# The experts' stage of a transformer kernel on one core: 40 loaded expert units in slot order against 32 units, of which eight serve two token slots

## The reference, cut to what matters

```python
g_sel = argmax(softmax(t @ w_rg + b_rg))           # one of 4 groups per token
e_prob = softmax((t @ w_re + b_re)[g_sel])         # 8 experts in the group
top_p, top_i = top_k(e_prob, 2)
combine = g_p * top_p / sum(top_p)                 # per token, over 32 experts
for e in range(32):                                # expert width 256
    hid = silu(t @ w_gate[e]) * (t @ w_up[e])
    out += combine[:, e] * (hid @ w_down[e])
```

## Time and profile before

| | |
|---|---|
| median of 3 runs (lowest to highest) | 2045.34 us (2042.76 to 2045.85) |
| the profiled execution | 2042.77 us, its span 2041.0 us |
| mean granted clock of PE in it | 0.989 of full |
| PE / POOL busy over the span | 96% / 65% |
| DMA over the span | 473.92 MB, mean 232 GB/s |
| from the first gather to the last unit's silu | 246.1 to 680.9 us |

### The profile page before, as it was taken

How to read it: one execution, slowest core, us unless ns; L and a number is a source line. 1 busy time by engine, 2 the same in 40 slices (tenths; PEclk the granted TensorE clock), 3 DMA queues, 4 the chain that set the end, 5 groups by cost and what they waited for, 6 DMA issues and landing times.

```text
span 2041.0 us, 34520 instructions
## 1 busy us (share of the span) xinstructions
PE 1968.1 (96%) x13902; PEld 1768.6 (87%) x13902; DVE 1020.0 (50%) x2154; ACT 824.4 (40%) x874; POOL 1329.9 (65%) x310
## 2 busy tenths in 40 slices
PE   6999889999999999999999999899999999999998
PEld 4879767667676799999999769799999999999998
DVE  6767474558565465455336334453335334654212
ACT  4343354444444553334434332443344333434332
POOL 5727157776768668777775412377777777777884
PEclk8999899999999999999999999999999999999999
DMA  8537198989898655666665402156665666655552
GB/s 354 214 124 289 67 374 349 376 345 368 355 375 336 230 224 210 244 239 225 241 241 205 153 33 104 60 215 242 247 239 204 233 233 244 229 221 192 185 185 83
DMA packets 67414, 473.92 MB, mean 232 GB/s; under 512 B 8064, under 2 KB 9184, under 8 KB 10208
## 3 DMA queue, kind: packets, MB, share of 16 engines
q1 hardware_dynamic: 65344, 466.82, 60.2%
q10 hardware_dynamic: 1952, 5.44, 0.7%
HBM read 471.18 MB, written 1.05 MB: 231 GB/s over the span
## 4 chain that ended last, share of the span: by engine, by line
PE 48%; issue 23%; POOL 19%; DMA 6%; DVE 1%; ACT 1%; SPq 0%; POOLq 0%; ACTq 0%; DVEq 0%
POOL W L632 15%; PE bank L703 11%; PE bank L705 11%; PE bank L704 11%; DMA raw<-in_pages 6%; PE bank L1197 4%; POOL YC L685 2%; PE bank L709 2%; PE bank L711 2%; PE bank L710 2%; PE bank L737 1%; ACT W L1616 1%; PE bank L728 1%; PE bank L748 1%; POOL W L685 1%
## 5 line engine op out<-in xcount | busy, mean ns | idle before, releaser
L632 POOL TENSOR_TENSOR W<-raw,W 128x2048 fp32r<-128x2048 f32 x220 | 1014.0, 4614 | 518.9 <-ACT W L1494 518.8
L703 PE MATMUL bank<-YH,W 128*128 128x256 f32 x1936 | 551.2, 285 | 1.1 <-POOL W L632 0.8
L705 PE MATMUL bank<-YH,W 128*128 128x256 f32 x1936 | 547.7, 283 | 0.0
L704 PE MATMUL bank<-YL,W 128*128 128x256 f32 x1936 | 547.6, 283 | 0.0
L1494 ACT ACTIVATE W<-raw 128x2048 fp32r<-128x2048 f32 x220 | 420.1, 1909 | 302.0 <-PE bank L705 275.6
L703 PEld LDWEIGHTS bank<-YH,W 128*128 128x128 f32 x1936 | 371.0, 192 | 3.9 <-POOL W L632 1.2
L704 PEld LDWEIGHTS bank<-YL,W 128*128 128x128 f32 x1936 | 371.3, 192 | 0.4 <-issue 0.2
L705 PEld LDWEIGHTS bank<-YH,W 128*128 128x128 f32 x1936 | 371.2, 192 | 0.0
L1828 DVE SCALAR_TENSOR_TENSOR bank<-mraw,CA,bank 128x256 f32<-128x256 f32 x696 | 329.1, 489 | 20.3
L1925 DVE TENSOR_TENSOR bank<-bank,SIL 128x256 f32<-128x256 f32 x110 | 47.6, 433 | 540.9 <-ACT SIL L1513 540.9
L703 PE MATMUL bank<-HH,W 128*128 128x256 f32 x880 | 249.7, 284 | 0.5 <-DVE HL L1927 0.4
(11 more groups left out here) (353 smaller groups left out, 3159.5 us busy)
## 6 DMA issues: line engine op xcount, KB each, us to landing
raw<-in_pages SPq DMA_DIRECT2D x299, 1024.0 KB, 4.9
mraw<-in_mpages SPq DMA_DIRECT2D x98, 1024.0 KB, 6.9
R<-in_pages SPq DMA_DIRECT2D x24, 1024.0 KB, 5.8
XR<-in_pages SPq DMA_DIRECT2D x17, 1024.0 KB, 5.5
R<-in_mpages SPq DMA_DIRECT2D x4, 1024.0 KB, 16.3
HT<-in_acts ACTq DMA_DIRECT2D x1, 1024.0 KB, 14.1
CT<-in_mpages SPq DMA_DIRECT2D x1, 1024.0 KB, 19.4
raw<-in_mpages SPq DMA_DIRECT2D x1, 1024.0 KB, 25.1
```

The source lines that it names most:

```text
L632: nc.gpsimd.tensor_tensor(WL[:, p % SLOTS, :], raw[:, p % SLOTS, :], WH[:, p % SLOTS, :].bitcast(f32), ALU.subtract).then_inc(s_lo, 1)
L703: mm(out, w[0], x[0], start=start, stop=False, skip_group_check=True)
L704: mm(out, w[0], x[1], start=False, stop=False, skip_group_check=True)
L705: return mm(out, w[1], x[0], start=False, stop=stop, skip_group_check=True)
```

## The change

The slots are numbered anew. The group with the most tokens always has slots 0 and 1; the other three groups have slots 2, 3 and 4. There are 32 units, and `JOBS` lists 40 pairs of unit and slot: units 0 to 7 run for slot 0 and then slot 1 (jobs 0 to 15), units 8 to 31 for one slot each (jobs 16 to 39). The tokens of slots 0, 1 and 2 are gathered in the start, so three gathered slots are held. Slot 1 sums its output in banks 5 and 6. The modulation pages move: one in each job from 1 to 15, then one in every second job from 17 to 35. For the first 15 their product is put in bank `TURN`, and `turn_hid` of jobs 1 to 15 waits until `mod_take` has read it. Slots 0 and 1 are scattered together, with eight matmuls in place of four. The core of the diff:

```diff
-NUNIT = GSLOTS * NE8
-MOD_UNITS = [_u for _u in range(36) if _u % 10 not in (0, 4, 7)]
+NUNIT = NEXP
+JOBS = [(_u, _j) for _u in range(NE8) for _j in range(2)] + [(_u, 1 + _u // NE8) for _u in range(NE8, NUNIT)]
+NJOB = len(JOBS)
+DONE_AT = {_u: _t for _t, (_u, _j) in enumerate(JOBS)}
+MOD_JOBS = list(range(1, 16)) + list(range(17, 37, 2))
...
-        EARLY = [(u, part) for u in range(2) for part in range(2)]
+        EARLY = [(0, 0), (0, 1)]
...
-        BY_VECTOR = [(2, 1)] + [(u, 1) for u in range(3, 36) if u not in MOD_UNITS]
-        BY_POOL = [(u, part) for u in range(2, NUNIT) for part in range(2) if (u, part) not in BY_VECTOR]
+        BY_VECTOR = [(u, 1) for u in range(NE8 + 2, NUNIT - 2, 2)]
+        BY_POOL = [(u, part) for u in range(1, NUNIT) for part in range(2) if (u, part) not in BY_VECTOR]
...
+        def mod_bank(m, i=0):
+            return PS[TURN if isinstance(i, int) and 0 <= m + 1 - MOD_AT["moe"] < 15 else MODB]
...  (SP)
-                    if u > 2:
-                        sp.wait_ge(s_gdown, u - 2)
+                    if u > 2:
+                        sp.wait_ge(s_gdown, DONE_AT[u - 3] + 1)
...
+                if u > 1:
+                    for t in range(NJOB):
+                        if JOBS[t][0] == u - 1 and t in MOD_JOBS:
+                            mod_page(MOD_AT["moe"] + MOD_JOBS.index(t))
...  (PE)
+            def turn_hid(t):
+                pe.wait_ge(s_ghid, t + 1)
+                pe.wait_ge(s_ght, t)
+                if t == 0:
+                    pe.wait_ge(s_auxd, 6)
+                if t in MOD_JOBS and t <= 15:
+                    pe.wait_ge(s_modev, MOD_AT["moe"] + MOD_JOBS.index(t))
                 for j in range(2):
                     last = nc.tensor.transpose(PS[TURN][:, j * P:(j + 1) * P], HID[:, j, :], IDENT[:])
                 last.then_inc(s_gturn, 1)
...
-            gather(0, 0)
-            gather(0, 1)
+            for j in range(2):
+                gather(j, 0)
+                gather(j, 1)
             aux(0)
+            aux(1)
+            for t in range(NJOB):
+                u, j = JOBS[t]
+                e = u % NE8
+                if t == 0:
+                    early_gate_up(0)
+                    early_gate_up(1)
+                    gather(2, 0)
+                    gather(2, 1)
+                    aux(2)
                 else:
+                    gate_up(t, range(0, KD // 2))
+                    turn_hid(t - 1)
+                    gate_up(t, range(KD // 2, KD))
+                    down(t - 1)
+                if j > 1 and 1 <= e <= 4:
+                    scatter(j - 2, e - 1)
+                if t in MOD_JOBS:
+                    k = MOD_JOBS.index(t)
                     mod_product(MOD_AT["moe"] + k - 1, 0, 1 if k < MOE_ADA else 2)
...  (ACT)
                 if u > 1:
-                    act.wait_ge(s_gu, u - 1)
+                    act.wait_ge(s_gu, DONE_AT[u - 2] + 1)
...
+                if t == 0:
+                    gathered_hi(2, 0)
+                    gathered_hi(2, 1)
+                    expert_split(1, 0)
+                    expert_split(1, 1)
+                if DONE_AT[u] == t and u + 2 < NUNIT:
                     expert_split(u + 2, 0)
                     expert_split(u + 2, 1)
...  (DVE)
+            aux_copy(1)
+            onehot(2)
+                if t in MOD_JOBS:
+                    k = MOD_JOBS.index(t)
                     vectors = (0,) if k < MOE_ADA else (1, 2)
                     mod_sum(MOD_AT["moe"] + k, vectors)
                     mod_take(MOD_AT["moe"] + k - 1, 0, len(vectors))
```

More of the change, by code:

```diff
@@ L125, in build @@
         HT = sb("HT", [P, KD, S])
+        with nc.sbuf_tensor("CTR", [P, KD * S], f32r) as CTR:
+            pass
         CT = sb("CT", [P, KD, S])
@@ L678, in _ @@
                 .then_inc(sem("iota"), 1)
-            for u in range(2, NUNIT):
+            for u in range(1, NUNIT):
                 for part in range(2):
@@ L1107, in aux, with to_tokens @@
                 for t in range(TB):
-                    last = mm(ps[:, S:S + NE8], EM[:, t, :], CW8[:, t, :], start=(t == 0), stop=(t == TB - 1),
+                    last = mm(ps[:, S:S + NE8], EM[j % 2][:, t, :], CW8[:, t, :], start=(t == 0), stop=(t == TB - 1),
                               skip_group_check=True)
                 last.then_inc(s_aux, 1)
-            def to_tokens(ps, j, r):
+            def to_tokens(ps, slots, r):
                 for b in range(2):
                     k = 2 * r + b
[L1115 to L1118, removed]
-                return last
@@ L1121, in scatter @@
-            def scatter(j, r):
+                    for j in slots:
+                        for part in OS[j]:
+                            last = mm(ps[:, b * S:(b + 1) * S], part[:, k * P:(k + 1) * P], ET[:, j % 3, :],
+                                      start=(j == slots[0] and part is OS[j][0]), stop=(j == slots[-1] and part is OS[j][1]),
+                                      skip_group_check=True)
+                return last
+            def scatter(g, r):
+                slots = (0, 1) if g == 0 else (g + 1,)
@@ L1187, in turn_hid, with down @@
                 last.then_inc(s_gturn, 1)
-            def down(u):
-                pe.wait_ge(s_ght, u + 1)
+            def down(t):
+                u, slot_j = JOBS[t]
+                pe.wait_ge(s_ght, t + 1)
                 pe.wait_ge(sem(f"expert_down_in_{u % 2}"), 16 * (u // 2 + 1))
-                if u % NE8 == 0 and u:
-                    pe.wait_ge(s_osl, 2 * (u // NE8))
+                if u % NE8 == 0:
+                    if slot_j == 1:
+                        pe.wait_ge(s_xl, 6)
+                    if slot_j > 1:
+                        pe.wait_ge(s_osl, 2 if slot_j == 2 else 2 * slot_j)
                 w = down_page(u)
@@ L1208, in _ @@
             pe.wait_ge(sem("tokens_copied"), 4)
-            gather(0, 0)
-            gather(0, 1)
+            for j in range(2):
+                gather(j, 0)
+                gather(j, 1)
             aux(0)
-            for u in range(NUNIT):
-                if u > 1:
-                    gate_up(u, range(0, KD // 2))
-                    turn_hid(u - 1)
-                    gate_up(u, range(KD // 2, KD))
-                    down(u - 1)
-                else:
-                    early_gate_up(u, 0)
-                    if u:
-                        turn_hid(u - 1)
-                    early_gate_up(u, 1)
-                    if u:
-                        down(u - 1)
-                if u in MOD_UNITS:
-                    k = MOD_UNITS.index(u)
+            aux(1)
+            for t in range(NJOB):
+                u, j = JOBS[t]
+                e = u % NE8
[5 more added lines that the diff above has]
+                    aux(2)
+                else:
+                    gate_up(t, range(0, KD // 2))
[6 more added lines that the diff above has]
+                    k = MOD_JOBS.index(t)
                     mod_product(MOD_AT["moe"] + k - 1, 0, 1 if k < MOE_ADA else 2)
-                j, e = u // NE8, u % NE8
-                if j and 1 <= e <= 4:
-                    scatter(j - 1, e - 1)
-                if j + 1 < GSLOTS:
+                if 1 < j < GSLOTS - 1:
                     if e in (5, 6):
@@ L1235, in _ @@
                         aux(j + 1)
-                if u == NUNIT - 3:
-                    pe.wait_ge(s_scd, 4 * (GSLOTS - 1))
+                if t == NJOB - 3:
+                    pe.wait_ge(s_scd, 4 * (GSLOTS - 2))
                     norm(2)
-            turn_hid(NUNIT - 1)
-            down(NUNIT - 1)
+            turn_hid(NJOB - 1)
+            down(NJOB - 1)
             def mid_norm(name, u, n):
@@ L1684, in _ @@
             after(PA["ctx_ff"] - SLOTS)
-            hid_copy(NUNIT - 1)
+            hid_copy(NJOB - 1)
             after(PA["ctx_ff"] - 1)
```

291 lines of the change are left out of this document (148 added, 143 removed).

## The result

The changed kernel took 2031.18 us in the median of 8 runs (2029.74 to 2036.25), the kernel before 2042.53 in 8 runs beside it (2038.91 to 2046.38): a ratio of **0.9948, 95% interval 0.9935 to 0.9961**, 11.4 us faster. Two more sets gave 0.9955 [0.9938, 0.9973] and 0.9948 [0.9930, 0.9966], that is 7.8 and 11.2 us. One run of the kernel before, in the set of part 4, took 3893 us and is left out of every figure.

A forecast was written before the change was run, and what follows sets the result against it. PE was taken as the bound. Start +5.8, work -7.0 and waits 12.3 in place of 16.3 (-4.0) gave -5.2 us: from the median 2045.3 to 2040.1 us, range 2033 to 2049.

The forecast's parts named there:

- What bounds, and what a gain can be: Experts' loop: PE is the bound; nothing done to the loads can give more than 16.3 us there.
- rival D: Loads are the bound: 25.2 MB fewer would give 72 us, 1973 us in all; chance 0.01.
- Rival C: Modulation bank holds each of the first 15 jobs: slower, +22 us, 2067 (2060 if pages less late); chance 0.12.
- A: Jobs 16 to 39 starve as before: waits of 10 us in place of 5.5, 2044.6, no change; chance 0.3.
- B: Waits of the second part fall from 5.5 us to nothing: -10.7 us, 2034.6; chance 0.15.
- The added wait: Jobs 12 to 15: `turn_hid` waits for `mod_take` of its own job, 1.4 us each, 5.6 us in all.
- The first split of POOL: Job 1: POOL ends unit 1's two parts after PE wants them, a wait of 1.2 us, once.
- `onehot` at nothing while POOL is idle: Start: the onehot of slot 2 costs nothing, as POOL is idle then.
- Work -7.0: Loop: PE's work falls to 385.2 us, 7.0 less, moved to the start and not saved.
- the waits of before 16.3: Loop of the kernel before: 411.9 us less 392.2 of work and 3.4 of norm leaves 16.3 us of waiting.
- Start +5.8: Start: job 0's `down` begins near 274.6 us against 268.77, 5.8 us later, after more gathers and `aux`.
- The stages behind begin earlier by as much; their work is unchanged: After the experts' stage: later stages shift by the same -5.2 us and gain nothing more.

The follow-up runs named there:

- part 4: Half of each `down` page loaded: in the changed kernel from unit 8 on, 2029.78 us; in the kernel before for all units, 2033.01 us.
- e1_take: Changed kernel with `mod_take` put in the middle of the next `mod_sum` in jobs 12 to 15: 2026.93 us, ratio 0.9916; again 2028.37 us, 0.9925.
- e5: Changed kernel with `mod_take` mid-sum in jobs 12 to 15, plus ACT splitting unit 1 ahead of its copies of slot 2's gathers: 2036.06 us, ratio 0.9962.
- part 1: Both kernels again, unchanged, for more profiles: changed kernel 2034.77 us in 8 runs; kernel before 2038.16 and 2040.39 us in one run each.
- e4_before_halfdown: Kernel before with only the first half of every unit's `down` page loaded, 21 MB fewer: 2033.01 us in 8 runs, ratio 0.9948.

## Why the prediction was wrong

The mechanism in the experts' stage was right. Three things were not: what the stages outside would give was put at nothing, the start was priced too dear, and the base of the median was too high.

**What bounds, and what a gain can be: right.** PE sets the pace. 25.2 MB less (448.74 MB moved, 449 forecast) moved the loop by 11.3 us and not by 72, so rival D is out. Rival C too: jobs 2 to 11 are all 9.62. A and B are the two ends of the second part's waits, 10 and 0; they came to 7.0, between A and the 5.5 of the forecast. A's main argument, the same load per us, did not quite hold: from 422 to 672 us the queues moved 326 GB/s at a share of 0.83, where the forecast had 351 (344 and 0.87 in before, from 422 to 681).

**The added wait: right.** 1.28 us of idle time and the restart, 5.75 in all against 5.6, by e1_take. **The first split of POOL: right**, 1.51 against 1.2. **`onehot` at nothing while POOL is idle: right**, and by e5 that cover was worth some 7 us (34.0 against 26.8 from the first gather to the first `down`). The forecast had no price for it: its 1 to 2 us are for `out_low` at job 16, where nothing was lost (9.25 in job 16).

**Work -7.0, and the waits of before 16.3: the sizes were off, the sum not.** I took 0.67 for a product of one vector from 6.84. In that row the first `gate_up` matmul starts 0.59 us after the product. Another unit of before has 0.37, and in after it is 0.36 in each of jobs 2 to 11:

```profile
282.09 0.50 PE L728 MATMUL bank<-ONES,MACC 128*128 128x1 f32 x4
282.68 0.47 PE L709 MATMUL bank<-W,YH 128*128 128x512 f32 x1
...
348.99 0.50 PE L728 MATMUL bank<-ONES,MACC 128*128 128x1 f32 x4
349.36 0.48 PE L709 MATMUL bank<-W,YH 128*128 128x512 f32 x1
```

```profile
295.30 0.50 PE L748 MATMUL bank<-ONES,MACC 128*128 128x1 f32 x4
295.66 0.48 PE L728 MATMUL bank<-W,YH 128*128 128x512 f32 x1
```

The row I priced from very likely held 0.2 us of waiting that no bracket shows. The product costs 9.62 - 9.17 = 0.45 in after. If it costs the same in before, that kernel had 11 x 0.22 = 2.4 us less of work and 18.7 of waits, and after 382.8 of work, 3.4 of norm and 14.4 of waits: 1.6 at job 1, 5.75 in jobs 12 to 15, and 7.0 in jobs 16 to 38 (247.09 less the forecast's work), where I had 5.5 (bounds 0 to 10). The two misses, -2.2 and +1.5, nearly cancel: the loop came out at 400.64 for 400.9.

**Start +5.8: too much by 1.3, the step that failed in the stage.** From the residual to the first `down` it is +4.5 (45.45 against 40.99). Four gathers, two `aux`, two gathers more, `aux(2)` and a whole `gate_up` took 26.94 us from the first gather where I had 28.1. The six gathers make nearly all of the miss: the first four took 9.9 us (10.5 forecast), the other two with `aux(2)` 4.15 (4.7). I priced a gather at 2.03; the last two took 1.79 each, which is the 1.78 of the earlier trace rows. `gate_up` took 5.85 for 6.0, and the rest came out within 0.1. The remaining 0.2 lie ahead of the first gather.

**"The stages behind begin earlier by as much; their work is unchanged": the step that failed most.** The work is unchanged, but not its time. In the mean of three profiles of each kernel the stage gives 7.0 us (452.4 against 445.5). The medians give 11.4, 7.8 and 11.2, a mean of 10.1. The rest, some 3 us, goes with the granted clock. In the profiles it can be placed: ahead of the stage (1.1 us in the mean) and behind it (1.2), each time with a fall of the clock that one execution has and another of the same kernel has not (part 1). In the runs it can be priced: the 54 of before in the later sets have a mean clock of 0.9904 and a mean span of 2041.6, the 22 of after 0.9925 and 2031.0. At equal clock the spans differ by 6.7 us (0.991), 8.2 (0.992) and 8.0 (0.993), not by 10.6, near what the stage gives. In the runs of before the clock is 0.986 to 0.994 over the span, and the three slowest of the set of experiment 1 (spans of 2047.9 to 2048.6) have 0.986 or 0.987; in the 22 runs of after it is 0.990 to 0.994. One fall in the loop, behind unit 5's wait, I had seen and counted in one profile; I did not ask how often the others come. The fall behind unit 5 is in two of three profiles of before and in none of after, and it is part of the stage's 7.0. Why the falls of other stages come less often after the change stays open. It need not be the new order: e4_before_halfdown has the order of before, and gains 7.5 us in its stage (444.95) and 11.1 in its median.

**On the median: the base was off too.** I set the forecast on the median of three runs, 2045.34; larger sets of the same kernel gave 2042.53, 2042.57, 2044.13, 2042.18 and 2043.02. Of the 8.9 us between 2040.1 and 2031.18 some 2.8 are that, 1.6 the stage, and the other 4.5 lie outside it, where I had nothing.

## What to carry to other kernels

Price an added piece from the smallest of its instances, not from the first: a small wait behind it leaves no mark, and it makes work look dearer and waits cheaper. A new wait of 1.3 us that PE meets four times is worth a look before the load that it makes possible: taking `mod_take` into the middle of the sum gave 7.8 and 3.5 us in two sets, for a few lines, and no later version is faster than it by more than the intervals. And where the granted clock falls in one execution and not in the next, as here, the medians differ by what no single profile shows: compare several profiles from a mark ahead of the change, and runs at equal clock, before a difference is given to the change.

## What the runs showed of the hardware

**DVE can be held by POOL for the length of POOL's instruction.** It is not only the `onehot` of e5. In the kernel after, DVE's low part takes 2.28 us alone and 4.31 beside POOL: it is issued at 451.75, POOL ends at 453.90, and it ends at 456.06, 2.2 later. The same holds for all ten of the loop: three with POOL idle take 2.28 or 2.29 us, and the seven that begin beside an instruction of POOL end 2.14 to 2.16 us behind its end.

```profile
431.63 2.28 DVE L2304 TENSOR_TENSOR W<-raw,W 128x2048 fp32r<-128x2048 f32 x1
...
449.27 4.63 POOL L704 TENSOR_TENSOR W<-raw,W 128x2048 fp32r<-128x2048 f32 x1
...
451.75 4.31 DVE L2304 TENSOR_TENSOR W<-raw,W 128x2048 fp32r<-128x2048 f32 x1 [1.43 <-ACT W L1648]
```

DVE's sums, with one input in SBUF and one in PSUM, keep their length: 0.52 us a step for one vector and 0.45 for two, at 272.51 and 461.94 beside POOL as elsewhere without it. The Trainium skill (SBUF — State Buffer, Who interferes with whom) says so: an operation of DVE with two inputs in SBUF, or a `tensor_scalar` that meets the conditions of a two-port mode, contends with an instruction of GpSimd that reads SBUF; the one issued first has the shared ports for its whole length, and the other is blocked fully. The trace agrees, with the seven low parts and the 4.43 us for two columns. So a low part moved from POOL to DVE is done behind the one that POOL has begun, not beside it, and I had not weighed that.

**The granted clock falls in stretches that the change does not touch, and not in every execution** (0.91 or 1.00 from 1160 to 1200 us, with 36.2 us of PE busy in both; 0.83 or 1.00 from 100 to 120 us in two executions of the kernel before). The Trainium skill (TensorE: Matmul & The Clock Gate, What's actually happening) says that the number of slow matmuls of a kernel varies from run to run. The runs here agree, with the whole span at 0.986 to 0.994 for one kernel.
